# A two-block transformer kernel: the last three units of the second output projection taken in two lots of 256 tokens

## The chip, the cores and the metric

The kernel runs on one core of a Trainium2 chip. The metric is device time in microseconds (us), the median of three runs. The engines are TensorE (PE, with its weight loads as PEld), VectorE (DVE), ScalarE (ACT), GpSimd (POOL) and SyncE (SP), whose queue issues nearly all transfers. Each engine works through its own list of instructions in order, and semaphores tie them together.

## The reference, cut to what matters

A first block (pooling mixer and norm) is followed by a block of two attention layers, A and B. The change touches only the end of layer B:

```python
y = (o * jax.nn.silu(g)) @ w_out                                  # (1024, 1024) @ (1024, 1024)
h = layer_norm_2(DEEPNORM_ALPHA * h + gate[:, None, :] * y, ln_g[i], ln_b[i])

def layer_norm_2(x, g, b):
    mu = mean(x, -1); var = mean((x - mu) ** 2, -1)
    return (x - mu) * rsqrt(var + 1e-5) * g + b
```

The norm runs over the 1024 features of a token. All data are float32.

## The kernel before

**Products.** Activations lie with features on partitions: `act_buf[:, o, t]` is feature tile `o` (of eight) over all tokens. A weight matrix is cut into units of 128 output features. SP loads a unit raw into one of `W_SLOTS = 3` slots, once the product that used the slot is done; POOL splits it (`split`: a cast `w_hi`, L726, then a difference `w_lo`, L728), and PE waits for both parts (`w_split`). One product of a unit with a stretch of tokens (a "chunk") is 8 steps of 3 matmuls (L911 to L913), 24 in all, summed in one of two PSUM banks `pj`; a chunk's index picks the bank, and `pj_free` (the wait `consumed`) says that DVE has read it.

**The second output projection** (`output_projection(1)`). First the feature tiles are made for tokens 0 to 511 (and for tiles 0, 1 and 2 over all tokens). Then come the chunks in `AGAIN[1]`: feature tiles 3, 4, 5, 6, 7 for tokens 512 to 1023, each one chunk of 512 columns, each with its unit loaded again. Units `BO_UNIT + 8` to `BO_UNIT + 12` are these five. Below they are called products 0, 1, 2, ... in the order of `AGAIN[1]`.

After each product DVE adds it, times the gate, to the residual (`residual_sum`, L1935); SP has loaded that residual into `res` in one of two places (`load_res`, one group of `RES` at a time, after the group two before it was consumed).

**The norm.** A "row" is 128 tokens turned so that tokens lie on partitions. Row `t` takes: PE turns eight tiles into a PSUM place (`to_rows(2, t)`, L920; two places, so it waits until row `t - 2` was normalised); DVE `statistics` (L1655 to L1658); POOL `root` (L751, raises to the power -1/2); DVE `scales` (L1664); ACT `normalise_last` writes `x_hat` (L1499); DVE `normalise_last` multiplies by the row `g` (L1697); POOL `add_row` adds `b` (L893); SP `store_out` sends the row out. Rows 0 to 3 hold tokens 0 to 511 and are turned one after each of products 0 to 3. Rows 4 to 7 need all feature tiles of tokens 512 to 1023, and come after the last product and its sum.

**The order on POOL** is written out at the end of its list and is not touched by the diff:

```python
        for n in range(BO_UNIT + W_SLOTS, BO_UNIT + KT + W_SLOTS):
            split(n)
        pool.wait_ge(rows_loaded, 16 * 2)
        root(2, 0)
        split(BO_UNIT + KT + W_SLOTS)
        root(2, 1)
        add_row(0)
        split(BO_UNIT + KT + W_SLOTS + 1)
        for t in range(1, S // P - 1):
            root(2, t + 1)
            add_row(t)
```

So the split of unit `BO_UNIT + 12`, the last one (feature tile 7), stands behind `add_row(0)`, and that one behind DVE's `normalise_last(0)`.

**The order on DVE** before, with the products' sums: sum 0; statistics 0, sum 1, scales 0; normalise_last(0), statistics 1, sum 2, scales 1; normalise_last(1), statistics 2, sum 3, scales 2; normalise_last(2), statistics 3, sum 4, scales 3; then statistics 4, normalise_last(3), scales 4, and for each further row the statistics of the next, normalise_last of this one, scales of the next.

Of the kernel before, what the change touches and what calls it, by code (L numbers as in the profile page):

```python
# [2 lines left out]

# [1 line left out]

# [8 lines left out]
P = 128  # L14
D = 1024
S = 1024
C = 256
TC = S + C
KT = D // P
HALF = 512  # L20
# [16 lines left out]
W_SLOTS = 3  # L37
# [8 lines left out]
OUT_AGAIN = ((0, 1, 3, 4, 5, 6, 7), (3, 4, 5, 6, 7))  # L46
OUT_UNITS = tuple(KT + len(again) for again in OUT_AGAIN)
L1_LAST = (GROUPS - 1) * L1_UNITS
A_UNIT = GROUPS * L1_UNITS + 4
AO_UNIT = A_UNIT + 20  # L50
B_UNIT = AO_UNIT + OUT_UNITS[0]
BO_UNIT = B_UNIT + 4 * PAIRS
ALL_UNITS = BO_UNIT + OUT_UNITS[1]
# [7 lines left out]
ALL_CHUNKS = LAT_CHUNKS + [(S, C)]  # L61
# [8 lines left out]
LN0 = (0, 8, 18)  # L70
# [39 lines left out]
Chunk = namedtuple("Chunk", "index kind pair n unit t0 tn k0 steps")  # L110
# [26 lines left out]
def out_chunks(layer, unit, index):  # L137

    early, first = ((0, 2), (0, 1))[layer], ((0, 2), (0,))[layer]
    order = [(o, n) for o in range(2) for n in early] if layer == 0 else [(o, n) for n in early for o in range(2)]  # L140
    row = [("p", o, n, o, 0, KT - 1) for o, n in order] + [("o", 2, n, 2, 0, KT) for n in first]
    row += [("o", 2, 1, 2, 0, KT)]
    row += [("o", o, n, o, 0, KT) for o in range(3, KT) for n in first]
    row += [("o", o, 1, KT + i, 0, KT) for i, o in enumerate(OUT_AGAIN[layer])]
    return [Chunk(index + i, kind, o, n, unit + u, *ALL_CHUNKS[n], k0, steps) for i, (kind, o, n, u, k0, steps) in enumerate(row)]


def last_steps(layer):
# [10 lines left out]
STAGES, OUTS = (A_STAGES, B_STAGES), (AO_CHUNKS, BO_CHUNKS)  # L159
# [1 line left out]
LAST = tuple(last_steps(layer) for layer in range(2))  # L161

LAST_END = {c.unit: c.index + 1 for row in LAST for c in row}
AGAIN = tuple(row[-len(again):] for row, again in zip(OUTS, OUT_AGAIN))

RES = tuple([[c for c in row if c.kind == "o" and c.unit == u] for u in sorted({c.unit for c in row if c.kind == "o"})]
            for row in OUTS)


def residual_counts():  # L170
# [116 lines left out]
def build(nc, a):  # L287
# [198 lines left out]
    def consumed(eng, c):  # L486

        after(eng, pj_free[c.index % 2], c.index // 2 + 1)
# [80 lines left out]
    def _(sp):  # L569
# [19 lines left out]
        for g in range(GROUPS):  # L589
            for u in range(L1_UNITS + (4 if g == GROUPS - 1 else 0)):  # L590
                n = g * L1_UNITS + u
# [43 lines left out]
        def store_out(i):  # L635

            sp.wait_ge(out_ready, i + 1)
            sp.dma_start(a["out"][i], out_tile[:, i % OUT_SLOTS, :]).then_inc(out_stored[i % OUT_SLOTS], 16)
# [9 lines left out]
        def load_out(layer):  # L648

            sp.wait_ge(logit_done, STEP0[layer] + 2 * PAIRS * TILES[layer])  # L650
            for n in range(2):
                load_res(layer, n)
            if layer == 1:
                sp.wait_ge(gated, TILE0[1] + PAIRS * TILES[1])
                for dst, src in ((g_row, "ln_g3"), (b_row, "ln_b3")):
                    sp.dma_start(dst[:, :], bass.AP(tensor=a[src].tensor, offset=0, ap=[[0, P], [1, D]])).then_inc(rows_loaded, 16)
            for n in range(OUT_UNITS[layer]):
                unit, done = (AO_UNIT, BO_UNIT)[layer] + n, n - 2
                if unit + W_SLOTS < ALL_UNITS:
                    load_unit(unit + W_SLOTS)  # L660
                if done >= 0 and done + 2 < len(RES[layer]):
                    for c in RES[layer][done]:
                        consumed(sp, c)
                    load_res(layer, done + 2)
                if layer == 1 and n >= KT + 2:
                    store_out(n - KT - 2)

        store_residual(0, 0)
        store_residual(0, 1)
# [24 lines left out]
        for j in range(PAIRS - 1):  # L694
            n = B_UNIT + 4 * (j + 1) + W_SLOTS
# [12 lines left out]
        load_y(1, y_more, LAT_CHUNKS[1:], BO_CHUNK)  # L708
        load_out(1)

        for i in range(3, S // P - 1):
            store_out(i)
        store_last()
        for s in range(OUT_SLOTS):
# [192 lines left out]
    def _(pe):  # L907
# [15 lines left out]
        def to_rows(ln, i):  # L923

            n, t = LN0[ln] + i, LN_TILES[ln][i]
            if n >= ROW_SLOTS:
                pe.wait_ge(ln_norm, n - ROW_SLOTS + 1)
            turn_tiles(ps_rows[n % ROW_SLOTS], [act_buf[:, k, t * P:(t + 1) * P] for k in range(KT)]).then_inc(ln_turned, 1)
# [38 lines left out]
        for g in range(GROUPS):  # L967
            unit = g * L1_UNITS
# [244 lines left out]
        def output_projection(layer):  # L1213


            n = len(EARLY[layer])
            third = OUTS[layer][n:n + (2, 1)[layer]]
            for c in third[1 - layer:]:
                work(layer, [(c, 0, KT - 1)])
            for c in LAST[layer][:2]:  # L1220
                last_step(layer, c)
            for c in third:
                last_pair_there(layer, c)
                work(layer, [(c, KT - 1, KT)])
            for c in LAST[layer][2:]:
                last_step(layer, c)
            for c in OUTS[layer][n + len(third):-len(AGAIN[layer])]:
                last_pair_there(layer, c)
                work(layer, [(c, 0, c.steps)])
            whole = [c for c in OUTS[layer] if c.kind == "o"]  # L1230
            for i, c in enumerate(AGAIN[layer]):
                work(layer, [(c, 0, KT)])
                if i == 0:
                    for l in whole:
                        if l.pair == KT - 1 and l.n != 1:
                            consumed(pe, l)
                if layer == 0:
                    if i:
                        to_columns(1, i - 1)
                    for t in (range(2), (2,), (3,), (4,), (5,), (), ())[i]:  # L1240
                        to_rows(1, t)
                elif i <= 3:
                    to_rows(2, i)

        start_a()
        attention(0)
# [3 lines left out]
        output_projection(1)  # L1250
        for c in BO_CHUNKS[-2:]:
            consumed(pe, c)
        for i in range(4, S // P):
            to_rows(2, i)
    @block.scalar
    def _(act):
# [273 lines left out]
    def _(dve):  # L1530
# [120 lines left out]
        def statistics(n):  # L1651

            s, rows = n % ROW_SLOTS, ps_rows[n % ROW_SLOTS]
            dve.wait_ge(ln_turned, n + 1)
            dve.bn_stats(stats[:, s, 0:6], rows[:, 0:HALF])  # L1655
            step(dve.bn_stats(stats[:, s, 6:12], rows[:, HALF:D]))
            step(dve.bn_aggr(mean_var[:, s, :], stats[:, s, :]))
            dve.tensor_scalar(var_eps[:, s:s + 1], mean_var[:, s, 1:2], LN_EPS, None, ALU.add).then_inc(ln_var, 1)  # L1658

        def scales(n):  # L1660

            s = n % ROW_SLOTS
            dve.wait_ge(ln_rstd, n + 1)
            dve.tensor_scalar(neg_mean[:, s:s + 1], mean_var[:, s, 0:1], rstd[:, s:s + 1], -1.0, ALU.mult,  # L1664
                              ALU.mult).then_inc(ln_scaled, 1)
# [21 lines left out]
        def normalise_last(i):  # L1687

            n, place = LN0[2] + i, i % 2
            if i == 0:  # L1690
                dve.wait_ge(rows_loaded, 16 * 2)
            dve.wait_ge(ln_norm, n + 1)
            if i >= OUT_SLOTS:
                dve.wait_ge(out_stored[i % OUT_SLOTS], 16)
            out = out_tile[:, i % OUT_SLOTS, :]
            if i < S // P - 1:
                dve.tensor_tensor(out, x_hat[:, place, :], g_row[:, :], ALU.mult).then_inc(out_scaled, 1)  # L1697
                return
            for h in range(2):
                half = slice(h * HALF, (h + 1) * HALF)  # L1700
                step(dve.tensor_tensor(out[:, half], x_hat[:, place, half], g_row[:, half], ALU.mult))
                dve.tensor_tensor(out[:, half], out[:, half], b_row[:, half], ALU.add).then_inc(last_ready, 1)
# [234 lines left out]
        def output_sums(layer):  # L1937

            dve.wait_ge(y_split, sum(LOW_COUNT[:layer + 1]))
            n = len(EARLY[layer])  # L1940
            third = OUTS[layer][n:n + (2, 1)[layer]]
            for c in LAST[layer][:2] + third + LAST[layer][2:]:
                residual_sum(layer, c)
            for c in OUTS[layer][n + len(third):-len(AGAIN[layer])]:
                residual_sum(layer, c)
            for i, c in enumerate(AGAIN[layer]):
                if layer == 0 and i:
                    normalise(1, i - 1)
                if layer == 1 and i >= 2:
                    normalise_last(i - 2)  # L1950
                if layer == 1 and i:
                    statistics(LN0[2] + i - 1)
                if layer == 0 and i == 5:
                    low_part(1, 0, 0, 1)
                residual_sum(layer, c)
                if layer == 1 and i:
                    scales(LN0[2] + i - 1)
                if layer == 0 and i >= 5:
                    low_part(1, 0, *((2, 3), (4, 5, 6, 7))[i - 5])

# [15 lines left out]
        start_b()  # L1976
        attention(1)
        output_sums(1)
        statistics(LN0[2] + 4)
        normalise_last(3)  # L1980
        scales(LN0[2] + 4)
        for i in range(4, S // P):
            if i + 1 < S // P:
                statistics(LN0[2] + i + 1)
# [122 lines left out]
```

## Time and profile before

| | us |
|---|---|
| median of three runs | 2037.91 (2035.29 to 2041.16) |
| profiled execution, first to last instruction (its span) | 2034.1 |
| around the span (median less span) | 3.8 |
| PE busy in the span | 1978.8 |
| start of the sum of the last product (product 4) | 2010.30 |
| from there to the end of the span | 23.8 |

The profile has no other time for the profiled execution than its span. Columns of the timeline: start in us from the span's start, duration in us, engine, line, operation, output and inputs, shapes, count, and in brackets the engine's idle time before it and what ended it.

### The profile page before, as it was taken

The numbers are of one execution on the slowest core, as the hardware profiler recorded it, in microseconds if no ns is written. First come the engines' busy times: TensorE is split into PE (matmuls) and PEld (weight loads), VectorE is DVE, ScalarE is ACT, GpSimd is POOL, SyncE is SP. The second block draws the span as 40 slices with busy tenths as digits, with TensorE's granted clock in tenths as the row PEclk, the third lists the DMA queues.
The fourth block names the chain that finished last, engine by engine and source line by source line (L and its number), as shares of the span: only waits on it lengthen the run. The fifth ranks groups of instructions, "written<-read, shape, count | busy, mean of one in ns | idle before, by whom it ended". The sixth has DMA issues, their size and how long they took to land.

```text
span 2034.1 us, 36964 instructions
## 1 busy us (share of the span) xinstructions
PE 1978.8 (97%) x14892; PEld 1639.4 (81%) x14892; DVE 1074.3 (53%) x2229; ACT 829.5 (41%) x1641; POOL 834.3 (41%) x624
## 2 busy tenths in 40 slices
PE   7999999999999999999999999999999999999996
PEld 6888888888887788888888788778888888888784
DVE  5556566666855665556656723734334343344626
ACT  4110110110126565556667610735555555555501
POOL 3433333333346622212122635545435435435746
PEclk9999999999999999999999999999999999999998
DMA  4332232332222401111001433221111111111343
GB/s 159 135 103 88 99 103 74 114 101 75 93 93 75 146 22 35 35 35 35 22 25 35 135 97 112 79 85 51 43 51 53 43 53 52 43 52 54 109 135 119
DMA packets 51063, 156.02 MB, mean 77 GB/s; under 512 B 5584, under 2 KB 9296, under 8 KB 50768
## 3 DMA queue, kind: packets, MB, share of 16 engines
q1 hardware_dynamic: 49888, 152.40, 22.7%
q8 instruction: 120, 1.97, 0.4%
q10 hardware_dynamic: 1008, 1.27, 0.2%
q14 instruction: 47, 0.39, 0.1%
HBM read 132.94 MB, written 20.71 MB: 76 GB/s over the span
## 4 chain that ended last, share of the span: by engine, by line
PE 65%; DVE 2%; POOL 2%; issue 2%; ACT 2%; DMA 1%; DVEq 0%; SPq 0%; POOLq 0%; ACTq 0%
PE psum L911 16%; PE psum L912 14%; PE psum L913 14%; PE psum L1099 8%; PE psum L1046 7%; PE psum L1062 5%; PE psum L920 1%; POOL w_lo L728 1%; DMA w_raw<-weights_in 1%; POOL rstd L751 0%; PE psum L1073 0%; ACT logits L1380 0%; DVE logits L1797 0%; POOL out_tile L893 0%; DVE u_lo L1684 0%
## 5 line engine op out<-in xcount | busy, mean ns | idle before, releaser
L911 PE MATMUL psum<-u_hi,w_hi 128*128 128x512 f32 (+1 forms) x1440 | 543.5, 377 | 2.6 <-DVE u_lo L1684 2.6
L912 PE MATMUL psum<-u_lo,w_hi 128*128 128x512 f32 (+1 forms) x1440 | 524.8, 364 | 0.0
L913 PE MATMUL psum<-u_hi,w_lo 128*128 128x512 f32 (+1 forms) x1440 | 524.3, 364 | 0.0
L726 POOL CAST w_hi<-w_raw 128x1024 fp32r<-128x1024 f32 x140 | 156.4, 1117 | 823.3 <-DMA w_raw<-weights_in 823.3
L728 POOL TENSOR_TENSOR w_lo<-w_raw,w_hi 128x1024 fp32r<-128x1024 f32 x140 | 348.4, 2489 | 11.2
L911 PEld LDWEIGHTS psum<-u_hi,w_hi 128*128 128x128 f32 x1440 | 271.5, 189 | 55.1 <-DVE u_lo L1684 4.4
L913 PEld LDWEIGHTS psum<-u_hi,w_lo 128*128 128x128 f32 x1440 | 271.8, 189 | 44.7
L912 PEld LDWEIGHTS psum<-u_lo,w_hi 128*128 128x128 f32 x1440 | 272.1, 189 | 38.4
L1380 ACT ACTIVATE logits<-logits,neg_max 128x640 f32<-128x640 f32 (+2 forms) x288 | 226.1, 785 | 69.7 <-DVE neg_max L1797 68.1
L1389 ACT ACTIVATE logits<-logits,row_rec 128x640 f32<-128x640 f32 (+1 forms) x288 | 218.0, 770 | 0.0
L1403 ACT ACTIVATE prob_t<-psum 128x320 f32<-128x320 f32 (+1 forms) x288 | 118.7, 412 | 241.1 <-PE psum L1062 240.8
L911 PE MATMUL psum<-x_hi,w_hi 128*128 128x512 f32 x512 | 200.2, 391 | 12.9 <-DVE x_lo L1539 11.7
L912 PE MATMUL psum<-x_lo,w_hi 128*128 128x512 f32 x512 | 199.7, 390 | 0.0
L913 PE MATMUL psum<-x_hi,w_lo 128*128 128x512 f32 x512 | 199.7, 390 | 0.0
L1575 DVE CUSTOM_DVE_ANT_0 psum<-w_ada,psum,vecs 128x1024 f32<-128x1024 f32 x96 | 123.6, 1288 | 62.7 <-issue 60.5
L1062 PE MATMUL psum<-ident,logits 64*128 64x64 f32 x2624 | 143.2, 229 | 7.4 <-DVE prob_t L1819 4.9
L1062 PEld LDWEIGHTS psum<-ident,logits 64*128 64x128 f32 x2624 | 115.0, 138 | 41.8 <-issue 36.6
L1797 DVE CUSTOM_DVE_ANT_0 logits<-psum,a_mask,sink_neg 128x640 f32<-128x640 f32 (+2 forms) x160 | 124.0, 775 | 40.7 <-PE psum L1046 39.6
L1819 DVE COPY prob_t<-psum 128x320 f32<-128x320 f32 (+1 forms) x288 | 131.6, 457 | 12.7 <-PE psum L1062 5.2
L1797 DVE CUSTOM_DVE_ANT_0 logits<-psum,bias 128x640 f32<-128x640 f32 x128 | 105.1, 822 | 44.8 <-PE psum L1046 26.7
L1285 ACT ACTIVATE u_pad<-psum 128x512 f32<-128x512 f32 x32 | 19.0, 598 | 267.2 <-PE psum L913 262.0
L851 POOL TENSOR_TENSOR bias<-tab,col_mask 128x384 f32<-128x384 f32 x96 | 92.6, 965 | 77.3 <-DMA tab<-bias_tab_in 75.8
(165 smaller groups left out, 3005.0 us busy)
## 6 DMA issues: line engine op xcount, KB each, us to landing
w_raw<-weights_in SPq DMA_DIRECT2D x140, 512.0 KB, 3.5
w_ada<-w_ada_in SPq DMA_DIRECT2D x48, 512.0 KB, 3.5
residual<-act_buf SPq DMA_DIRECT2D x4, 2048.0 KB, 7.5
tab<-bias_tab_in SPq DMA_DIRECT2D x16, 496.5 KB
res<-residual SPq DMA_DIRECT2D x26, 256.0 KB, 3.5
y_all<-staged SPq DMA_DIRECT2D x24, 256.0 KB, 4.7
act_buf<-x_t_in SPq DMA_DIRECT2D x8, 512.0 KB, 13.0
staged<-a_y SPq DMA_DIRECT2D x6, 640.0 KB, 2.9
```

Of the source, the lines that this page charges most:

```text
L726: pool.tensor_copy(w_hi[:, slot, :], w_raw[:, slot, :]).then_inc(w_hi_done, 1)
L728: pool.tensor_tensor(w_lo[:, slot, :], w_raw[:, slot, :], w_hi[:, slot, :].bitcast(F32), ALU.subtract).then_inc(w_split, 1)
L911: pe.matmul(out, wh, xh, start=first, stop=False)
L912: pe.matmul(out, wh, xl, start=False, stop=False)
L913: return pe.matmul(out, wl, xh, start=False, stop=last)
L1046: mm = pe.matmul(ps_score[h][:, P + c:P + c + n], q[r, t * P:(t + 1) * P], keys(k[r, :]), start=m == 0, stop=m == 2)
L1062: tr = pe.transpose(ps_pt[n][:, c * HD:(c + 1) * HD], logits[s % SLOTS][r, c0 + c * P:c0 + (c + 1) * P], ident[r, r])
L1099: mm = pe.matmul(out[r, :], v[:, tile, r], prob_t[:, g % 2, h, c, :], start=c == 0, stop=c == len(tiles) - 1)
L1380: act.activation(lg[:, c0:end], lg[:, c0 + 1:end + 1], ACT.Exp, scale=-1.0, bias=neg_max[:, n:n + 1], accum_out=row_sum[:, n:n + 1]).then_ ...
L1389: act.activation(pr, pr, ACT.Copy, scale=row_rec[:, n:n + 1]).then_inc(prob_scaled, 1)
L1797: dve.tensor_tensor_reduce(logits[n][:, c0 + 1:KEYS + 1], ps_score[h][:, P + c0:P + KEYS], add, -1.0, start, ALU.add, ALU.min, neg_max[:, ...
L1819: dve.tensor_copy(prob_t[:, g % 2, h, 0:n, HD:P], ps_pt[1][:, 0:n * HD].rearrange("p (t q) -> p t q", q=HD)).then_inc(pt_dve, 1)
```

## The change

Products 0 and 1 (feature tiles 3 and 4) stay as they are. Tiles 5, 6 and 7 are each done in two chunks of 256 columns: products 2, 3, 4 are tiles 5, 6, 7 over tokens 512 to 767, products 5, 6, 7 the same tiles over tokens 768 to 1023. Their three units stay in the three slots, so no weight is loaded or split again. PE turns row 0 after product 0, row 1 after product 1, row 2 after product 3, row 3 after product 5, row 4 after product 6 (with a wait until products 3 and 4 are consumed), and rows 5 to 7 after the last. DVE's order becomes: sum 0; statistics 0, sum 1, scales 0; statistics 1, sum 2, scales 1; normalise_last(0), sum 3; statistics 2, sum 4, scales 2; normalise_last(1), sum 5; statistics 3, sum 6, scales 3, normalise_last(2); statistics 4, sum 7, scales 4, normalise_last(3); then the rest as before from row 5's statistics on. On SP, the residual groups become 14 in place of 11 (the last six of 256 columns), and no row is sent out before the last residual load is issued; before, rows 0 to 2 were sent inside that loop. For layer A the same code gives the same chunks and order as before.

```diff
@@ out_chunks
-    row += [("o", o, 1, KT + i, 0, KT) for i, o in enumerate(OUT_AGAIN[layer])]
-    return [Chunk(index + i, kind, o, n, unit + u, *ALL_CHUNKS[n], k0, steps) for i, (kind, o, n, u, k0, steps) in enumerate(row)]
+    whole = len(OUT_AGAIN[layer]) - (0, W_SLOTS)[layer]
+    again = list(enumerate(OUT_AGAIN[layer], KT))
+    row += [("o", o, 1, u, 0, KT) for u, o in again[:whole]]
+    row = [(kind, o, n, u, *ALL_CHUNKS[n], k0, steps) for kind, o, n, u, k0, steps in row]
+    row += [("o", o, 1, u, t0, C, 0, KT) for t0 in (HALF, HALF + C) for u, o in again[whole:]]
+    return [Chunk(index + i, kind, o, n, unit + u, t0, tn, k0, steps) for i, (kind, o, n, u, t0, tn, k0, steps) in enumerate(row)]
@@
-AGAIN = tuple(row[-len(again):] for row, again in zip(OUTS, OUT_AGAIN))
-
-RES = tuple([[c for c in row if c.kind == "o" and c.unit == u] for u in sorted({c.unit for c in row if c.kind == "o"})]
+AGAIN = tuple(row[-len(again) - (0, W_SLOTS)[layer]:] for layer, (row, again) in enumerate(zip(OUTS, OUT_AGAIN)))
+
+RES = tuple([list(group) for _, group in groupby((c for c in row if c.kind == "o"), key=lambda c: (c.unit, c.n == 1 and c.t0 > HALF))]
             for row in OUTS)
+
+LAST_ROWS = {1: 0, 2: 1, 4: 2, 6: 3, 7: 4}
+ROWS_AFTER = {0: (0,), 1: (1,), 3: (2,), 5: (3,), 6: (4,)}
@@ SP, load_out
-            for n in range(OUT_UNITS[layer]):
+            for n in range(max(OUT_UNITS[layer], len(RES[layer]))):
                 unit, done = (AO_UNIT, BO_UNIT)[layer] + n, n - 2
-                if unit + W_SLOTS < ALL_UNITS:
+                if unit + W_SLOTS < (AO_UNIT, BO_UNIT)[layer] + OUT_UNITS[layer] or layer == 0:
                     load_unit(unit + W_SLOTS)
...
-                if layer == 1 and n >= KT + 2:
-                    store_out(n - KT - 2)
@@ SP
-        for i in range(3, S // P - 1):
+        for i in range(S // P - 1):
             store_out(i)
@@ PE, output_projection
-                elif i <= 3:
-                    to_rows(2, i)
+                else:
+                    if i == 6:
+                        for l in AGAIN[1][3:5]:
+                            consumed(pe, l)
+                    for t in ROWS_AFTER.get(i, ()):
+                        to_rows(2, t)
@@ PE, after the projection
-        for i in range(4, S // P):
+        for i in range(5, S // P):
             to_rows(2, i)
@@ DVE, output_sums
-                if layer == 1 and i >= 2:
-                    normalise_last(i - 2)
-                if layer == 1 and i:
-                    statistics(LN0[2] + i - 1)
+                if layer == 1 and i in (3, 5):
+                    normalise_last((i - 3) // 2)
+                if layer == 1 and i in LAST_ROWS:
+                    statistics(LN0[2] + LAST_ROWS[i])
                 if layer == 0 and i == 5:
                     low_part(1, 0, 0, 1)
                 residual_sum(layer, c)
-                if layer == 1 and i:
-                    scales(LN0[2] + i - 1)
+                if layer == 1 and i in LAST_ROWS:
+                    scales(LN0[2] + LAST_ROWS[i])
+                if layer == 1 and i >= 6:
+                    normalise_last(i - 4)
@@ DVE, after the sums
-        statistics(LN0[2] + 4)
-        normalise_last(3)
-        scales(LN0[2] + 4)
```

## Rows read from the trace of the kernel before

**Rows 1.** The page, busy time of PE, and by windows the stretch after the last product.
```profile
PE 1978.8 (97%) x14892; PEld 1639.4 (81%) x14892; DVE 1074.3 (53%) x2229; ACT 829.5 (41%) x1641; POOL 834.3 (41%) x624
...
2010.15:2034.10 23.95, 3.70 (x65) 3.04 (x64) 17.07 (x30) 6.02 (x5) 17.28 (x9) 0.59 0.33 131
```

**Rows 2.** Timeline, the rows after the last product: POOL, and DVE's last product sum.
```profile
2010.30 0.75 DVE L1935 SCALAR_TENSOR_TENSOR act_buf<-psum,ada,res 128x512 f32<-128x512 f32 x1 [0.98 <-PE psum L913]
...
2016.97 1.59 DVE L1697 TENSOR_TENSOR out_tile<-x_hat,g_row 128x1024 f32<-128x1024 f32 x1
2017.45 1.53 POOL L751 TENSOR_TENSOR rstd<-var_eps,minus_half 128x1 f32<-128x1 f32 x1
...
2025.05 1.53 POOL L751 TENSOR_TENSOR rstd<-var_eps,minus_half 128x1 f32<-128x1 f32 x1
```

**Rows 3.** Timeline of PE: a turn, product 2 (first and last matmul of 24), product 4's first.
```profile
1991.16 0.71 PE L920 MATMUL psum<-ident,act_buf 64*128 64x64 f32 x16
...
1991.81 0.50 PE L911 MATMUL psum<-u_hi,w_hi 128*128 128x512 f32 x1
...
1997.17 0.39 PE L913 MATMUL psum<-u_hi,w_lo 128*128 128x512 f32 x1
...
2004.44 0.50 PE L911 MATMUL psum<-u_hi,w_hi 128*128 128x512 f32 x1
```

**Rows 4.** Timeline, 256 columns in layer A: a chunk's first and last of 24 matmuls, one sum.
```profile
1039.05 0.39 PE L911 MATMUL psum<-u_hi,w_hi 128*128 128x256 f32 x1
...
1041.91 0.28 PE L913 MATMUL psum<-u_hi,w_lo 128*128 128x256 f32 x1
...
1204.67 0.48 DVE L1935 SCALAR_TENSOR_TENSOR act_buf<-psum,ada,res 128x256 f32<-128x256 f32 x1 [2.12 <-PE psum L913]
```

**Rows 5.** Timeline of DVE and ACT, products 1 to 3.
```profile
1992.24 1.21 ACT L1499 ACTIVATE x_hat<-psum,neg_mean,rstd 128x1024 f32<-128x1024 f32 x1 [52.23 <-DVE neg_mean L1664]
1993.55 1.23 DVE L1697 TENSOR_TENSOR out_tile<-x_hat,g_row 128x1024 f32<-128x1024 f32 x1 [1.34 <-ACT x_hat L1499]
1994.69 0.69 DVE L1655 BATCH_NORM_STATS2 stats<-psum 128x6 f32<-128x512 f32 x1
1996.26 0.15 DVE L1658 TENSOR_SCALAR var_eps<-mean_var 128x1 f32<-128x1 f32 x1
1997.66 0.75 DVE L1935 SCALAR_TENSOR_TENSOR act_buf<-psum,ada,res 128x512 f32<-128x512 f32 x1 [1.25 <-PE psum L913]
1999.81 1.66 DVE L1697 TENSOR_TENSOR out_tile<-x_hat,g_row 128x1024 f32<-128x1024 f32 x1 [1.27 <-ACT x_hat L1499]
```

**Rows 6.** Timeline of POOL, products 1 to 3: a split of before, then root, add_row and last split.
```profile
1989.72 2.38 POOL L728 TENSOR_TENSOR w_lo<-w_raw,w_hi 128x1024 fp32r<-128x1024 f32 x1
1996.49 0.56 POOL L751 TENSOR_TENSOR rstd<-var_eps,minus_half 128x1 f32<-128x1 f32 x1 [4.39 <-DVE var_eps L1658]
1997.02 2.39 POOL L893 TENSOR_TENSOR out_tile<-out_tile,b_row 128x1024 f32<-128x1024 f32 x1
1999.35 1.04 POOL L726 CAST w_hi<-w_raw 128x1024 fp32r<-128x1024 f32 x1
2000.47 3.25 POOL L728 TENSOR_TENSOR w_lo<-w_raw,w_hi 128x1024 fp32r<-128x1024 f32 x1
```

**Rows 7.** SP: the last unit's load, and the page's issues (size, median us to landing).
```profile
1991.26 0.33 SPq L577 DMA_DIRECT2D w_raw<-weights_in  x1
...
res<-residual SPq DMA_DIRECT2D x26, 256.0 KB, 3.5
```

**Rows 8.** Timeline of PE about an idle stretch in layer B, and the clock (last but two column).
```profile
1900.08 0.53 PE L1062 MATMUL psum<-ident,logits 64*128 64x64 f32 x10 [1.95 <-DVE prob_t L1819]
...
1902.32 0.63 PE L911 MATMUL psum<-u_hi,w_hi 128*128 128x512 f32 x1
1902.75 0.63 PE L912 MATMUL psum<-u_lo,w_hi 128*128 128x512 f32 x1
...
1901.50:1905.00 3.50, 3.50 (x10) 2.68 (x10) 2.68 (x6) 2.75 (x6) 3.42 (x4) 0.53 0.47 180
```

More of the change, by code:

```diff
@@ L2 @@
 from contextlib import ExitStack
+from itertools import groupby
 import numpy as np
```

## The prediction

> **What bounds the kernel now.** I read the page first: PE is busy 97% of the span, and the chain that ended last runs through PE nearly all the way, so an edit counts if it changes what PE waits for or what follows its last matmul. The windows of the end come next: in the 23.95 us after product 4, PE works 3.70 and DVE and POOL 17 each [rows 1]. The timeline there shows POOL as the bound: `root` of row 5 starts at 2017.45, that of row 7 at 2025.05, so a row costs 3.80 [rows 2]. A row is one `add_row` of 2.39 alone or less [rows 6] and one `root`. That root takes 1.53 where DVE's multiply by `g` is in flight and 0.56 where it is not, and the multiply takes 1.59 or 1.66 in place of 1.23 [rows 2, 5, 6]: they hold each other up. From the start of the last root at 2025.05 to the span's end are 9.05 us which the change leaves alone.
>
> Before that, PE runs products 0 to 4 without idling. The reader should look at how little slack there is: product 4 starts at 2004.44 [rows 3], and its weights' `w_lo`, started at 2000.47, ends at 2003.72 [rows 6]. It has 0.7 us to spare.
>
> **Part 1: chunks of 256 columns.** A 512 chunk runs from 1991.81 to the last start at 1997.17, 5.36 over 23 gaps, the first 0.1 longer: 0.229 apart, 5.49 per chunk. A 256 chunk takes 2.86 to its last start, likewise with a first gap 0.1 longer: 0.120 apart, 2.88 per chunk [rows 3, 4]. Weight loads, doubled by 72, stay hidden in layer A's like chunks, whose spacing is still about half. Three units cost 6 x 2.88 - 3 x 5.49 = +0.81 on PE. Bounds: layer A's spacing is the same instruction shape, so 0.7 to 1.0. Sums of 256 columns take 0.48 in place of 0.75 [rows 4, 5].
>
> **Part 2: DVE's new order, and what is behind it on POOL.** This decides. `normalise_last(0)` moves from ahead of statistics 1 to behind sum 2 and scales 1. Step by step: product 2 starts at 1991.81 as before, its last matmul at 1994.67, and the sum about 0.38 later (0.28 for that matmul, 0.10 as in the rows), 1995.05. With 0.40 for it and 0.13 for scales 1 (the pitch at which such instructions follow one another), `normalise_last(0)` starts at 1995.58 and ends at 1996.8. Before, it ran at 1993.55. `add_row(0)` can start at 1996.9; before it started at 1997.02, held by root 1 [rows 6]. So POOL is on the same schedule as before: `add_row(0)` to 1999.25, the cast to 2000.37, `w_lo` of the last unit.
>
> Duration of that `w_lo`: 3.25 before, with DVE's multiply at 1999.81 beside it, 2.38 without such a neighbour [rows 5, 6]. In the new order `normalise_last(1)` waits behind sum 4, so none runs. I take 2.38: weights ready at 2002.75, product 4 starts at 2002.85. (With 3.25 it would be 2003.7.) The load of that unit, issued at 1991.26 [rows 7], is there in time either way.
>
> But PE arrives much earlier. Product 3 follows product 2 at 1994.78 (its unit was split by 1992.1), last start 1997.54; turning row 2 takes until 1998.5 (0.65 from a turn to the next matmul in [rows 3], and 0.1 on either side). Product 4, feature tile 7, has had 5.7 us of shorter chunks ahead of it instead of 11.5 and finds no weights: **PE stands from 1998.5 to 2002.85, 4.35 us**. Behind it on PE stand products 5 to 7 and all later turns; everything waits.
>
> The Trainium skill has a rule on the pair above: "SBUF — State Buffer", engine access and the shared port pair, says that a VectorE operation with two SBUF inputs and a GpSimd operation that reads SBUF exclude each other for whole instructions. The trace agrees (1.66 for 1.23, 3.25 for 2.38). By that rule the split is at its short price here, because the multiply has gone away; without it the stall would be 0.87 longer.
>
> **Part 3: from product 4 on.** Product 4 to 2005.83, product 5 to 2008.70 (waits for nothing: tile 5's weights stay). Turning row 3 to 2009.44. Product 6 to its last start 2012.30, turning row 4 (products 3 and 4 long consumed; row 2 normalised by 2008) to 2013.16, product 7's last start 2016.02, and sum 7 at A = 2016.41, 6.11 later than the 2010.30 of before. The terms of the 6.11: stall 4.35, more matmul time 0.81, one turn moved ahead of the last product 0.85, first gaps after a stop 0.1.
>
> **Part 4: the rows after A.** One row fewer is turned after the last product, which read alone is worth 3.80. But products now come every 2.9 to 3.7 us and DVE and POOL are not done with the rows in time. Sum 6 starts at 2012.69; scales 3 and then `normalise_last(2)` at 2013.2 to 2014.45; `add_row(2)` to 2016.85; root 4 to 2017.4, so scales 4, which stands behind sum 7, starts at 2017.45 and not at 2016.8. `normalise_last(3)` to 2018.8, `add_row(3)` to 2021.2, root 5 at 2021.2 = A + 4.8. Before, root 5 started at 2010.30 + 7.15 [rows 2]. So the shorter end gives 2.35, not 3.80. After it, two rows at 3.80 and the 9.05 as before.
>
> **Part 5: SP.** Residual groups for products 6 and 7 are asked for after sums 4 and 5 (2006.5, 2009.4); at 3.5 to landing [rows 7], for half the bytes, they are there by 2010 and 2013, ahead of sums at 2012.7 and 2016.4. Hidden by 2.7 and more. The loads have one to two chunks each; if one came late it would delay a sum by the excess alone. Row 0 is sent after the last of these loads, at about 2009.5 in place of 1999.4; its place in `out_tile` is wanted by `normalise_last(4)` at about 2020. Cost nothing; it would cost from 10 us of delay on.
>
> **Part 6: the clock.** After PE idled 1.95 us in layer B, the granted clock was 0.53 of full, thus mostly 1.2 GHz, over 1901.50 to 1905.00, with matmuls of 512 columns 0.43 apart instead of 0.229 [rows 8]. The stall here is longer, 4.35 us, after a dense stretch, so I expect the same fall. If it lasts 3.4 us of product 4 and 5, at half of 0.43 per 256 columns (0.213, an estimate from that row) against 0.120, it loses 3.4 x (1 - 0.120/0.213) = 1.5. Bounds: nothing if the fall misses the work (a stretch that is low only while PE stands), 3.0 if it lasts twice as long. I take 1.5.
>
> By "TensorE: Matmul & The Clock Gate", section on the back-to-back issue gap, a matmul of 256 columns at the low clock takes 256/1.2 = 213 ns, an estimate of the Trainium skill's page; no row here has one of full height. The sum by it is the same.
>
> **Sum.** +6.11 - 2.35 = +3.76, with the clock +5.3. Span 2034.1 becomes about 2039.4; the median, 3.8 above the span, 2037.91 + 5.3 = 2043.2. That is +0.26%, just inside the 0.3% (6.1 us) that a measurement of this kernel can tell from no change.
>
> **The rivals.**
> *(a) Stall with one low-clock stretch or none, +3.8 to +5.3, within 0.3%.* For it: every step has a row. Against: 0.8 us is all that separates it from the next. Chance 0.56, with its own range 2040 to 2044.
> *(b) Slower by over 0.3%: the clock stays down after the stall.* Decides from a loss of 6.1 - 3.8 = 2.3 us on, which is 5.3 us of work at the low clock. Two stretches of 3.4 give 3.8 + 3.0 = +6.8, 2044.7; all 96 matmuls of products 4 to 7 low, 96 x 0.093 = 8.9, give +12.7, 2050.6. For it: idle over twice as long as that of [rows 8]. Against: there the clock was back within 4.9 us of work resumed. The same page's rule, that the gate goes by activity, leaves room for both. Chance 0.37.
> *(c) No stall, because the last split gets ahead after all.* Then A = 2016.41 - 4.35 = 2012.06, and -2.35 gives -0.6 (with the full 3.80 per row, -2.0): 2036 to 2037.3, within 0.3% too. Against it: POOL's order, which is untouched. Chance 0.04.
> *(d) Faster by over 0.3%.* Would need over 1.6 rows of 3.80 off the end; only one moves. Chance 0.03, for what I haven't seen.
>
> **Range and chances.** 2038.5 to 2047.5: down for a cheap stall (weights of tile 7 earlier, the short end worth its 3.80: 3.8 - 1.45 = +2.3, less the 1.5 us that the runs differ), up for two low stretches (+6.8) and a `w_lo` at its long price (+0.87) with the same spread. Faster 0.03, within 0.3% 0.60, slower 0.37.
>
> **What would show it.** In the trace after: 256-column matmuls 0.120 apart; PE idle about 4.4 us ahead of product 4, ended by POOL's `w_lo` of L728; that `w_lo` of 2.4 us starting near 2000.4, behind `add_row(0)` at 1996.9; a granted clock of 0.5 for some us after 2002; sum 7 at 2016.4 to 2018; three roots at 3.80 apart after it, the first 4.8 after sum 7. The prediction is wrong if PE doesn't idle there, if the clock stays low through products 5 to 7, or if a sum waits for a residual load.

## The result

The changed kernel takes 2042.57 us (median of 7 runs, 2040.33 to 2045.42), the kernel before 2037.32 (7 runs, 2035.29 to 2041.16). The ratio is 1.0022, 95% interval 1.0012 to 1.0033: 4.5 us by the ratio, 5.3 by the medians. The forecast was 2043.2, +0.26%, within 0.3%. The median lies in the range, and the change is in the likeliest case, a little slower and inside the 0.3% that was named.

The profiled execution took 2042.74 with a span of 2041.1, so 1.6 us lie around the span. Its lines are renumbered: L911 to L913 are now L917 to L919, `w_lo` L734, `root` L757, `add_row` L899, a product's sum L1945, the multiply by `g` L1707, a turn L926.

First, PE and its clock by windows. The columns after the window are its length, then busy time and count of PE, PEld, DVE, ACT and POOL, the granted clock as a share, the DMA share and GB/s.
```profile
1999.69:2001.60 1.91, 0.00 (x0) 0.00 (x0) 1.66 (x4) 0.00 (x0) 1.83 (x3) 1.00 0.25 69
2001.70:2004.00 2.30, 0.00 (x1) 0.03 (x1) 0.00 (x0) 0.00 (x0) 2.30 (x2) 0.51 0.00 0
2004.00:2008.50 4.50, 4.50 (x21) 4.50 (x22) 0.00 (x0) 0.00 (x0) 0.36 (x1) 0.50 0.01 4
2008.50:2019.40 10.90, 10.90 (x109) 10.30 (x108) 7.19 (x15) 2.42 (x2) 4.70 (x3) 1.00 0.31 120
2019.40:2041.10 21.70, 2.86 (x49) 2.38 (x48) 15.39 (x25) 4.81 (x4) 14.87 (x9) 0.57 0.37 146
```
PE does nothing in the first two windows. In the second its clock has already fallen to half (1.2 GHz), and in the third it works 21 matmuls at that level. Before, the same stage had no such window: from product 2's first matmul to the end of the last product PE was busy for all of the 18.34 us and at full clock, and the one long thin stretch was the end [rows 1]:
```profile
1991.81:2010.15 18.34, 18.34 (x107) 14.43 (x104) 11.30 (x21) 3.62 (x3) 11.06 (x9) 1.00 0.32 116
```

The timeline of PE shows what ended the idle time, the pitch of matmuls at the low clock, and the clock's return:
```profile
1998.98 0.71 PE L926 MATMUL psum<-ident,act_buf 64*128 64x64 f32 x16
...
2004.00 0.55 PE L917 MATMUL psum<-u_hi,w_hi 128*128 128x256 f32 x1 [4.31 <-POOL w_lo L734]
2004.35 0.41 PE L918 MATMUL psum<-u_lo,w_hi 128*128 128x256 f32 x1
...
2008.40 0.36 PE L919 MATMUL psum<-u_hi,w_lo 128*128 128x256 f32 x1
2008.61 0.28 PE L917 MATMUL psum<-u_hi,w_hi 128*128 128x256 f32 x1
2008.72 0.28 PE L918 MATMUL psum<-u_lo,w_hi 128*128 128x256 f32 x1
```
From 2004.35 to 2008.40 there are 19 gaps of 0.213; after it the gap is 0.12 again.

POOL's timeline of the same stage, to set beside [rows 6]:
```profile
1995.15 0.56 POOL L757 TENSOR_TENSOR rstd<-var_eps,minus_half 128x1 f32<-128x1 f32 x1 [1.91 <-DVE var_eps L1668]
1998.09 2.36 POOL L899 TENSOR_TENSOR out_tile<-out_tile,b_row 128x1024 f32<-128x1024 f32 x1 [2.38 <-DVE out_tile L1707]
2000.40 1.03 POOL L732 CAST w_hi<-w_raw 128x1024 fp32r<-128x1024 f32 x1
2001.51 2.34 POOL L734 TENSOR_TENSOR w_lo<-w_raw,w_hi 128x1024 fp32r<-128x1024 f32 x1
...
2019.97 0.55 POOL L757 TENSOR_TENSOR rstd<-var_eps,minus_half 128x1 f32<-128x1 f32 x1
2021.98 2.35 POOL L899 TENSOR_TENSOR out_tile<-out_tile,b_row 128x1024 f32<-128x1024 f32 x1 [1.46 <-DVE out_tile L1707]
2024.29 1.53 POOL L757 TENSOR_TENSOR rstd<-var_eps,minus_half 128x1 f32<-128x1 f32 x1
2025.79 2.34 POOL L899 TENSOR_TENSOR out_tile<-out_tile,b_row 128x1024 f32<-128x1024 f32 x1
2028.10 1.53 POOL L757 TENSOR_TENSOR rstd<-var_eps,minus_half 128x1 f32<-128x1 f32 x1
```
POOL stands 2.38 us for DVE's multiply of row 0, and the last split stands behind that. After the last product the roots of rows 5 and 6 are 3.81 apart, as in [rows 2].

Two spans differ by 7.0 us, more than the runs do. Part of it comes from far ahead of the change, so from here on times are counted from the first matmul of product 2 (1991.81 before [rows 3], 1993.03 after), and the end is taken to two decimals, 2034.13 and 2041.13:
```profile
1992.39 0.71 PE L926 MATMUL psum<-ident,act_buf 64*128 64x64 f32 x16
1993.03 0.38 PE L917 MATMUL psum<-u_hi,w_hi 128*128 128x256 f32 x1
```

| from product 2's first matmul, us | before | forecast | after |
|---|---|---|---|
| PE stands ahead of product 4 | 0 | 4.35 | 4.31 |
| product 4 starts | 12.63 | 11.04 | 10.97 |
| last sum starts | 18.49 | 24.6, with the clock 26.1 | 26.48 |
| root 5 after the last sum | 7.15 | 4.8 | 4.78 |
| end of the span | 42.32 | 47.6 | 48.10 |

### The profile page after: what moved, and what is told of

The parts are those of the page before. It is cut to its first block, busy times and chain, and to the rows that moved or that the text cites. A ratio compares the mean times of both kernels' runs of the same rounds, so it can differ in the third digit from the quotient of the medians.

```text
span 2041.1 us, 37121 instructions
## 1 busy us (share of the span) xinstructions
PE 1983.5 (97%) x14964; PEld 1646.9 (81%) x14964; DVE 1076.0 (53%) x2232; ACT 829.5 (41%) x1641; POOL 833.5 (41%) x624
## 4 chain that ended last, share of the span: by engine, by line
PE 64%; DVE 2%; POOL 2%; issue 2%; ACT 2%; DMA 1%; DVEq 0%; SPq 0%; POOLq 0%; ACTq 0%
PE psum L917 16%; PE psum L918 14%; PE psum L919 14%; PE psum L1105 8%; PE psum L1052 7%; PE psum L1068 5%; POOL w_lo L734 1%; PE psum L926 1%; DMA w_raw<-weights_in 1%; POOL out_tile L899 1%; POOL rstd L757 0%; PE psum L1079 0%; ACT logits L1390 0%; DVE logits L1807 0%; POOL w_hi L732 0%
## 5 line engine op out<-in xcount | busy, mean ns | idle before, releaser
L917 PE MATMUL psum<-u_hi,w_hi 128*128 128x512 f32 (+1 forms) x1464 | 549.2, 375 | 6.9 <-POOL w_lo L734 4.3
L918 PE MATMUL psum<-u_lo,w_hi 128*128 128x512 f32 (+1 forms) x1464 | 530.3, 362 | 0.0
L919 PE MATMUL psum<-u_hi,w_lo 128*128 128x512 f32 (+1 forms) x1464 | 530.0, 362 | 0.0
L734 POOL TENSOR_TENSOR w_lo<-w_raw,w_hi 128x1024 fp32r<-128x1024 f32 x140 | 348.7, 2491 | 11.2
L917 PEld LDWEIGHTS psum<-u_hi,w_hi 128*128 128x128 f32 x1464 | 277.6, 190 | 58.8 <-issue 5.3
L919 PEld LDWEIGHTS psum<-u_hi,w_lo 128*128 128x128 f32 x1464 | 277.8, 190 | 43.8
L918 PEld LDWEIGHTS psum<-u_lo,w_hi 128*128 128x128 f32 x1464 | 278.1, 190 | 37.7
L917 PE MATMUL psum<-x_hi,w_hi 128*128 128x512 f32 x512 | 200.4, 391 | 12.5 <-DVE x_lo L1549 10.9
L919 PE MATMUL psum<-x_hi,w_lo 128*128 128x512 f32 x512 | 199.9, 390 | 0.0
```

The source lines that it names most:

```text
L734: pool.tensor_tensor(w_lo[:, slot, :], w_raw[:, slot, :], w_hi[:, slot, :].bitcast(F32), ALU.subtract).then_inc(w_split, 1)
L917: pe.matmul(out, wh, xh, start=first, stop=False)
L918: pe.matmul(out, wh, xl, start=False, stop=False)
L919: return pe.matmul(out, wl, xh, start=False, stop=last)
```

## The experiments

All but e5, which starts from the kernel before, start from the changed kernel. Their traces are compared from product 2's first matmul, which takes out what differs ahead of it between executions. There is one trace of each kernel; e7, which is the changed kernel but for its stores, repeats all three of its figures within 0.04 us. The ratios are to the kernel before, whose runs were taken on the same chip. An interval of a ratio reaches 2 to 3 us to either side, so the timed runs can confirm differences of some 3 us and not those of 1 or 2, which rest on the traces.

| kernel | ratio to before (95%) | PE idle before product 4 | last sum | end |
|---|---|---|---|---|
| before | | 0 | 18.49 | 42.32 |
| changed | 1.0022 (1.0012 to 1.0033) | 4.31 | 26.48 | 48.10 |
| e1, last split first | 1.0001 (0.9992 to 1.0009) | 0.74 | 20.89 | 42.48 |
| e2, multiply 0 earlier | 1.0030 (1.0019 to 1.0041) | 2.88 | 25.75 | 47.36 |
| e3, PE kept at work | 1.0024 (1.0015 to 1.0032) | 0.37 | 24.54 | 46.15 |
| e4, e1 with row 4 late | 1.0015 (1.0006 to 1.0023) | 0.94 | 20.27 | 44.00 |
| e7, rows sent out early | 1.0026 (1.0017 to 1.0035) | 4.32 | 26.52 | 48.13 |
| e5, before with a new norm | 0.9981 (0.9973 to 0.9990) | 0 | 18.49 | 38.23 |
| e6, all together | 0.9954 (0.9940 to 0.9968) | 0 | 20.93 | 34.66 |

### e1: the last split ahead of add_row(0)

```diff
         root(2, 1)
-        add_row(0)
         split(BO_UNIT + KT + W_SLOTS + 1)
+        add_row(0)
```


> The changed kernel, but on POOL the last unit's split stands ahead of add_row(0), behind root 1. Theory (PE stands for the last split, and its clock falls for it): the idle time before product 4 goes from 4.3 to about 1.2 us (the split must still wait for its load and shares its time with DVE's multiply of row 0), the clock stays full, sum 7 comes about 21.4 us after product 2's first matmul instead of 26.5, and the time is about 5 us under the changed kernel, so within 1 us of the kernel before. Rival N (the 256-column chunks and the turn put among them cost the time on PE): the stall was only where slack showed; time stays within 1 us of the changed kernel, +4 to +5 over before. Rival S (rows sent out late on SP hold the end): no change from the changed kernel either.

PE's wait, the clock by windows from product 4 to the last sum, then POOL with DVE's multiply of row 0:
```profile
1998.92 0.36 PE L917 MATMUL psum<-u_hi,w_hi 128*128 128x256 f32 x1 [0.74 <-POOL w_lo L734]
...
1998.92:2012.42 13.50, 13.39 (x128) 12.79 (x128) 8.14 (x18) 2.41 (x2) 7.53 (x5) 1.00 0.29 108
```
```profile
1994.43 1.04 POOL L732 CAST w_hi<-w_raw 128x1024 fp32r<-128x1024 f32 x1 [0.23 <-DMA w_raw<-weights_in]
1995.29 1.26 DVE L1707 TENSOR_TENSOR out_tile<-x_hat,g_row 128x1024 f32<-128x1024 f32 x1
1995.55 3.23 POOL L734 TENSOR_TENSOR w_lo<-w_raw,w_hi 128x1024 fp32r<-128x1024 f32 x1
1998.74 2.38 POOL L899 TENSOR_TENSOR out_tile<-out_tile,b_row 128x1024 f32<-128x1024 f32 x1
```
The idle time is 0.74, the clock stays at full to the last product, and the end comes 5.62 us sooner than in the changed kernel. Exchanging two lines on POOL takes back what the change cost, to 0.16 us in the trace; the ratio of 1.0001 (up to 1.0009) leaves no room for rivals N and S at more than about 2 us together. The split is at its long price here, 3.23, because DVE's multiply of row 0 runs beside it.

### e2: the multiply of row 0 ahead of sum 2

```diff
-                if layer == 1 and i in (3, 5):
-                    normalise_last((i - 3) // 2)
+                if layer == 1 and i == 5:
+                    normalise_last(1)
                 if layer == 1 and i in LAST_ROWS:
                     statistics(LN0[2] + LAST_ROWS[i])
+                if layer == 1 and i == 2:
+                    normalise_last(0)
```


> The changed kernel, but DVE multiplies row 0 by g right after statistics 1, ahead of sum 2; POOL's order stays. Theory: add_row(0) starts 1.4 to 1.8 us earlier after product 2's start and so does the last split, PE idles 2.5 to 2.9 us instead of 4.3 before product 4, the clock may still fall; 1.4 us or more (to 3.4 if the clock holds) under the changed kernel. Rivals N and S: no change beyond 0.5 us.

PE idles 2.88 in place of 4.31, as expected, but only 0.74 of the 1.43 reach the end. The windows say why:
```profile
2001.90:2002.68 0.78, 0.00 (x0) 0.00 (x0) 0.33 (x2) 0.00 (x0) 0.78 (x1) 1.00 0.29 89
2002.68:2003.37 0.69, 0.00 (x1) 0.04 (x1) 0.00 (x0) 0.00 (x0) 0.69 (x2) 0.50 0.00 0
2003.37:2009.45 6.08, 6.08 (x28) 6.08 (x29) 0.52 (x2) 0.00 (x0) 0.36 (x1) 0.50 0.01 3
2009.50:2019.40 9.90, 9.90 (x101) 9.36 (x100) 6.62 (x14) 2.42 (x2) 4.65 (x3) 1.00 0.35 132
```
Twenty-eight matmuls ran at the low clock here, against 21, and 7 x 0.093 = 0.65 us is nearly all of the 0.69 that was lost on the way. Only 0.7 us of the low stretch fell into the stall, against 2.3 in the changed kernel: a shorter stall was paid for with more work at half rate. The expected 1.4 us was missed, since I had let the clock only help. The timed runs don't resolve 0.74 us; their ratio is if anything higher than the changed kernel's. The split is ready 9.39 us after product 2's start here, 2.5 sooner than in the kernel before (11.91), and PE still waits 2.88: its earlier arrival alone makes that wait.

### e3: PE kept at work through the stall

```diff
                     for t in ROWS_AFTER.get(i, ()):
                         to_rows(2, t)
+                    if i == 3:
+                        for _ in range(32):
+                            pe.matmul(bank(4)[:, 0:C], w_hi[:, c.unit % W_SLOTS, 0:P], u_hi[:, 0, HALF:HALF + C], start=True, stop=True)
```


> The changed kernel with 32 extra 256-column matmuls on PE (their result is not used) after row 2 is turned, which fill the time PE stands. Theory: product 4 still starts when POOL's w_lo is done, the idle time before it is under 0.6 us, the granted clock stays 1.00 through products 4 to 7, sum 7 comes 24.5 us after product 2's start instead of 26.5; 2.0 us under the changed kernel. If the low clock was no cost of its own: same as the changed kernel. If extra work on PE costs its time (rival N): 3.8 us over it.

By windows, the stall filled with matmuls, and products 4 to 7:
```profile
1998.90:2003.30 4.40, 4.07 (x34) 3.86 (x32) 1.66 (x4) 0.00 (x0) 4.32 (x4) 1.00 0.14 34
2003.30:2016.50 13.20, 13.17 (x128) 12.80 (x128) 7.18 (x15) 2.42 (x2) 4.88 (x4) 1.00 0.27 101
```
Product 4 starts 11.04 after product 2, as in the changed kernel (10.97), and still waits for the same `w_lo`. The clock holds at 1.00, and the last sum and the end come 1.94 and 1.95 sooner. That is the price of the low clock by itself, and it is what 21 matmuls at 0.213 in place of 0.120 come to (1.95). In the trace the extra work in the stall costs nothing and gains these 1.95 us. The timed runs don't show the gain: the ratio is 1.0024 against 1.0022, and intervals of 2 us to either side can't exclude it either.

### e4: row 4 turned late, on top of e1

```diff
-LAST_ROWS = {1: 0, 2: 1, 4: 2, 6: 3, 7: 4}
-ROWS_AFTER = {0: (0,), 1: (1,), 3: (2,), 5: (3,), 6: (4,)}
+LAST_ROWS = {1: 0, 2: 1, 4: 2, 6: 3}
+ROWS_AFTER = {0: (0,), 1: (1,), 3: (2,), 5: (3,)}
@@ PE, after the projection
-        for i in range(5, S // P):
+        for i in range(4, S // P):
@@ DVE, output_sums
-                if layer == 1 and i >= 6:
-                    normalise_last(i - 4)
+                if layer == 1 and i == 6:
+                    normalise_last(2)
@@ DVE, after the sums
+        statistics(LN0[2] + 4)
+        normalise_last(3)
+        scales(LN0[2] + 4)
```


> The kernel with the last split first, and row 4 turned after the last product, as the kernel before does, with statistics 4, multiply 3 and scales 4 after all sums. It prices the row moved ahead. Theory (POOL and DVE have a backlog, the row is worth 2.35 at the end less 0.85 for its turn on PE): 1.5 us slower than the kernel with the last split first. If a row moved ahead is worth its full 3.80: 3.0 us slower. If nothing (the end hangs on something else, such as the stores): no difference.

The end is 44.00 against e1's 42.48: 1.52 slower, as the 2.35 less 0.85 said, and half of the 3.0 that a row at its full price would give. Of the 1.52, 0.20 isn't the row's: the last unit's load came 0.20 later here (POOL's cast starts 3.10 after product 2, in e1 2.90), and PE waits 0.94 in place of 0.74. So the row that the change moves ahead is worth about 1.3 us in the trace. The timed ratios, 1.0015 against 1.0001, agree in sign and fit 1.3 as well as 3.0. The rest of the row's price is taken by the backlog: e1's root 4 starts at 2012.87, behind `add_row(2)`, and scales 4 waits for it.

### e7: rows sent out early

```diff
                     load_res(layer, done + 2)
+                if layer == 1 and n >= KT + 3:
+                    store_out(n - KT - 3)
...
-        for i in range(S // P - 1):
+        for i in range(3, S // P - 1):
             store_out(i)
```


> The changed kernel, but SP sends rows 0 to 2 out between the last residual loads, row 0 right after add_row(0) instead of 12.5 us later. Theory (stores hidden): no change, within 0.5 us of the changed kernel after product 2's start. Rival S (rows sent out late hold the end): 2 us or more under it.

48.13 against 48.10. Rival S is out: the stores are hidden.

### e5: another way through the norm, in the kernel before

```diff
 # DVE, normalise_last(i), right behind statistics of the same row (the scales, the order of the calls and the waits of root and statistics are left out)
-            dve.wait_ge(ln_norm, n + 1)
-                dve.tensor_tensor(out, x_hat[:, place, :], g_row[:, :], ALU.mult).then_inc(out_scaled, 1)
+            for h in range(2):
+                ins = dve.scalar_tensor_tensor(by_halves(out)[:, :, h, :], ps_rows[s][:, h * HALF:(h + 1) * HALF].rearrange("p (k n) -> p k n", n=HD),
+                                               mean_var[:, s, 0:1], by_halves(g_row[:, :])[:, :, h, :], ALU.subtract, ALU.mult)
+            ins.then_inc(ln_norm, 1)
 # ACT, normalise_last(i)
+            act.wait_ge(ln_norm, n + 1)
+            act.wait_ge(ln_rstd, n + 1)
+                act.activation(out, out, ACT.Copy, scale=rstd[:, place:place + 1]).then_inc(out_scaled, 1)
```


> The kernel before, with another way through the last norm: DVE makes (x - mean) * g from PSUM right behind the statistics of the same row (two instructions of 512 columns), ACT then scales by 1/std in place, POOL adds b. So DVE no longer reads two SBUF tensors per row, waits for no root, and PE waits for DVE alone for a PSUM place. The sum is the reference's in another order of multiplications. Theory (the end is bound by POOL and DVE holding each other up, 3.80 us per row): a row costs DVE about 3.1, POOL 2.9, roots of rows 5 to 7 are about 3.1 apart at 0.55 each, the end comes about 18.7 us after sum 4 instead of 23.8; 5 us under the kernel before. If the 3.80 were due to the latency of the chain and not to the pair: roots still 3.8 apart, no gain beyond 1 us.

POOL and DVE after the last product:
```profile
2020.99 0.55 POOL L753 TENSOR_TENSOR rstd<-var_eps,minus_half 128x1 f32<-128x1 f32 x1
2021.51 2.36 POOL L895 TENSOR_TENSOR out_tile<-out_tile,b_row 128x1024 f32<-128x1024 f32 x1
2023.94 0.55 POOL L753 TENSOR_TENSOR rstd<-var_eps,minus_half 128x1 f32<-128x1 f32 x1
```
```profile
2020.83 1.40 DVE L1701 SCALAR_TENSOR_TENSOR out_tile<-psum,mean_var,g_row 128x512 f32<-128x512 f32 x2
2022.15 0.69 DVE L1658 BATCH_NORM_STATS2 stats<-psum 128x6 f32<-128x512 f32 x1
```
DVE's product with `g` now reads one tensor from PSUM and one from SBUF, and it overlaps with `add_row` with neither stretched (1.40 for two halves, 2.36); root is back at 0.55 and a row costs 2.95 in place of 3.80. The edit also takes the root out of what DVE waits for, so alone it doesn't separate the pair from the latency of the chain. The rows before do: from `add_row` at 2015.14 to the one at 2026.55 POOL never idles, its `root` and `add_row` (1.53 and 2.34, the next starting 0.03 to 0.04 before the one before it ends) fill the 3.80. What e5 takes out is 0.98 of the root, of which 0.85 reach the row. So the pair of DVE and POOL was the bound of the end. From sum 4 to the end are 19.7 us instead of 23.8, a gain of 4.1 where 5.1 was expected; about 1 us of my sum for the last row was too short. The timed runs give 3.9 by the ratio (2.0 to 5.5) and 2.2 by the medians (2035.34 against 2037.53). The Trainium skill's "SBUF — State Buffer", section "Who interferes with whom", says that a VectorE instruction with two SBUF inputs contends with a GpSimd instruction that reads SBUF, and that one with at most one SBUF input (outside its two-port modes) doesn't; the traces agree on both sides of the rule, 3.80 a row with such a pair and 2.95 without.

### e6: the changed chunks, the new norm, and POOL's order

Beside the edits of e5 and e7 (PE's wait for products 3 and 4 also moves ahead by one product, and DVE's list follows the rows):
```diff
-LAST_ROWS = {1: 0, 2: 1, 4: 2, 6: 3, 7: 4}
-ROWS_AFTER = {0: (0,), 1: (1,), 3: (2,), 5: (3,), 6: (4,)}
+LAST_ROWS = {1: 0, 2: 1, 3: 2, 4: 3, 6: 4, 7: 5}
+ROWS_AFTER = {0: (0,), 1: (1,), 2: (2,), 3: (3,), 5: (4,), 6: (5,)}
 # POOL
-        root(2, 1)
         add_row(0)
+        root(2, 1)
         split(BO_UNIT + KT + W_SLOTS + 1)
```


> The changed kernel's chunks with the same new way through the norm, POOL's order add_row 0, root 1, last split, rows turned after products 0, 1, 2, 3, 5, 6 (rows 6 and 7 after the last), and rows 0 to 2 sent out between the last residual loads. Theory: the last split is done as PE wants it (idle under 1 us), the clock stays full, sum 7 comes about 21 us after product 2's first matmul, only rows 6 and 7 remain, the end comes about 33 to 35 us after product 2's start instead of 42.3 (before) and 48.1 (changed): 7 to 9 us under the kernel before. If the 256-column chunks have no use of their own, it is no faster than the kernel before with the new norm alone.

POOL about the last split, PE's first matmul of product 4, and two windows (products 2 to 7, and what follows):
```profile
1994.33 2.40 POOL L903 TENSOR_TENSOR out_tile<-out_tile,b_row 128x1024 f32<-128x1024 f32 x1
1996.68 0.56 POOL L761 TENSOR_TENSOR rstd<-var_eps,minus_half 128x1 f32<-128x1 f32 x1
1997.38 1.04 POOL L734 CAST w_hi<-w_raw 128x1024 fp32r<-128x1024 f32 x1
1998.51 2.40 POOL L736 TENSOR_TENSOR w_lo<-w_raw,w_hi 128x1024 fp32r<-128x1024 f32 x1
```
```profile
2001.68 0.39 PE L921 MATMUL psum<-u_hi,w_hi 128*128 128x256 f32 x1
```
```profile
1994.28:2015.21 20.93, 20.82 (x212) 19.81 (x208) 17.49 (x37) 4.66 (x5) 16.38 (x13) 1.00 0.43 158
2015.21:2028.90 13.69, 1.22 (x32) 1.11 (x32) 8.33 (x15) 3.58 (x4) 7.29 (x5) 0.67 0.39 154
```
The split ends at 2000.9, 0.8 ahead of PE. PE works through at full clock, and with two rows left the end takes 13.7 us after the last sum, not 23.8. Median 2029.35 against 2037.53, ratio 0.9954, 9.4 us by the ratio (6.5 to 12.2) and 8.2 by the medians, where 7 to 9 were expected: this kernel beats both. Against e5 (38.23) the chunks of 256 columns, with the order of rows that they allow and POOL's order, are worth 3.6 us in the trace. The three weren't taken one by one.

## Why the prediction was right

**Part 1, chunks of 256 columns.** 24 matmuls of 0.120, weight loads hidden: right.

**Part 2, the stall.** Right in place, cause and size: 4.31 against 4.35, ended by POOL's `w_lo`, itself 2.34 long and behind `add_row(0)`, with the multiply of row 0 as the start of the chain. e1 shows the cause by removing it, and e2 shows that it moves with DVE's multiply. The sum of the stall: before, the split was ready 0.72 ahead of PE; now it is ready 1.09 sooner after product 2's start (10.82 against 11.91), but PE comes 5.97 sooner (6.66 against 12.63).

**Part 3 and 4, the sum up to A and the shorter end.** A came 26.48 after product 2 with the low clock (24.54 without, e3; forecast 24.60). Root 5 came 4.78 after it (4.8). The two rows at 3.80 and the last 9.05 us (here 9.24) held. e4 puts the row moved ahead at about 1.3 net of its turn, where the terms gave 1.50.

**Part 5, SP.** Stores and residual loads hidden: right, by e7; no sum waited for a load.

**Part 6, the clock.** The mechanism was right, its size about a quarter too small: 1.5 was taken and 1.95 measured. The step is the length of the low stretch that meets work: I put 3.4 us, which is what the low stretch of [rows 8] lasted (1901.6 to 1905.0), and it was 4.6, out of 6.8 us from 2001.7 to 2008.5 of which 2.3 fell into the stall. The low stretch was twice as long as that of [rows 8], as in the upper bound, and a third of it met no work. Half of the 0.43 of that row is 0.215 per matmul and not 0.213, which changes nothing in the sum; 0.213 was measured. By the Trainium skill's "TensorE: Matmul & The Clock Gate", section "Back-to-back issue gap", 256 columns take 213 ns at 1.2 GHz; the trace agrees.

**The sum.** Measured from product 2: 4.31 + 1.95 + 0.81 + 0.85 - 2.21 = +5.71 (the 2.21 are the 2.37 of the earlier root 5 less 0.16 of a longer last stretch), and 5.78 in the trace; forecast 5.3. The median moved by 5.3, the ratio says 4.5, and their interval (2.4 to 6.7 us) holds all of these. That the medians differ by the very 5.3 of the forecast is luck. One remark on the frame: I set the median 3.8 us above the span, but the changed kernel's profiled execution took only 1.6 more than its span, and those of the kernel before, in the later runs, 1.8. The 3.8 mixed the spread between executions with what lies around a span; it did no harm because it stood on both sides.

Of the rivals, (b) was nearest: it needed 2.3 us lost to the low clock, and 1.95 were. (c) and (d) did not occur, and with the stall taken away (e1) the change comes to nothing, +0.16 in the trace where (c) gave -0.6: the 0.74 us that PE still waits are about the difference.

## What to carry to other kernels

When work on one engine is made to finish sooner, look at what the other engines' fixed orders put between now and the data it will then ask for: here a weight split with 0.7 us to spare stood behind two steps of a norm that nobody needed soon, and 5.7 us of shorter chunks ahead of it turned the spare into a stall. Put what the bound engine waits for ahead of what only the end needs, and count a row moved out of the tail at what the backlog leaves of it, not at its full price. Where two engines hold each other up, giving one of them an operand from PSUM can be worth nearly as much as an order: 4.1 us in e5, 5.6 in e1.

## What the runs showed of the hardware that was not expected

**A shorter stall bought little because the low clock stretch kept its length.** The granted clock was at 1.2 GHz for 6.83 us in the changed kernel (2001.70 to 2008.53) and for 6.82 in e2 (2002.68 to 2009.50), and had fallen 2.0 and 2.2 us after PE's last matmul. In the changed kernel PE idled 4.31 us and then ran 21 matmuls at that level; in e2 it idled 2.88 and ran 28. Half of the time won in the stall was lost again.

**The same idle time doesn't always lower the clock.** At the start of layer A, PE waits 1.81 us for DVE in both profiled executions. In that of the changed kernel the clock then fell; the same window in the kernel before stayed at full:
```profile
649.64 0.50 PE L917 MATMUL psum<-u_hi,w_hi 128*128 128x512 f32 x1 [1.81 <-DVE u_lo L1694]
...
650.00:653.40 3.40, 3.40 (x26) 2.63 (x25) 1.37 (x5) 1.97 (x3) 2.10 (x3) 0.51 0.00 0
```
```profile
649.72 0.50 PE L911 MATMUL psum<-u_hi,w_hi 128*128 128x512 f32 x1 [1.81 <-DVE u_lo L1684]
...
650.00:653.40 3.40, 3.40 (x36) 2.91 (x36) 1.45 (x5) 2.61 (x3) 2.01 (x3) 1.00 0.00 0
```
This lies far ahead of anything the diff touches. It explains the 1.2 us by which product 2 started later: the wait ends 0.08 us sooner in the changed kernel, and PE's second turn behind it starts 1.32 later (655.66 against 654.34). So it is one source of the spread of some 5 us between runs. PE has this wait of 1.8 us in all nine traces; the clock fell after it in five (changed, e2, e3, e5, e6) and stayed at full in four (before, e1, e4, e7).
